# Matmuls of the seven-product chains issued as pairs of 64-column products in the two column halves

## The reference

```python
proj = h @ w_in + b_in                                     # both layers, first model
ff = jnp.square(jax.nn.relu(x @ w_up[l])) @ w_down[l]
x = layer_norm(ALPHA * x + ff, ln2_g[l], ln2_b[l])
...
y_b = ssd_mixer(z, xbc, dt_raw, ...) @ w_o_ssd             # second model
mix = (jax.nn.sigmoid(g_a) * y_a + jax.nn.sigmoid(g_b) * y_b) @ w_out
u_gate, u_up = jnp.split(h2 @ w_ffn_in, 2, axis=-1)
f = (jax.nn.silu(u_gate) * u_up) @ w_ffn_out
```

## Time and profile before

| | |
|---|---|
| median of three runs | 1318.59 us (1318.37 to 1318.83) |
| span of the profiled execution | 1316.3 us (the page gives no other time of it) |
| TensorE matmul / weight load busy | 1304.7 us (99%) / 1169.0 us (89%), 9133 of each |
| VectorE / ScalarE / GpSimd busy | 943.1 (72%) / 427.1 (32%) / 178.0 us (14%) |
| DMA | 242.39 MB, mean 184 GB/s |

### The profile page before, as it was taken

How to read it: one execution, slowest core, us unless ns; L and a number is a source line. 1 busy time by engine, 2 the same in 40 slices (tenths; PEclk the granted TensorE clock), 3 DMA queues, 4 the chain that set the end, 5 groups by cost and what they waited for, 6 DMA issues and landing times.

```text
span 1316.3 us, 22023 instructions
## 1 busy us (share of the span) xinstructions
PE 1304.7 (99%) x9133; PEld 1169.0 (89%) x9133; DVE 943.1 (72%) x1602; ACT 427.1 (32%) x929; POOL 178.0 (14%) x164
## 2 busy tenths in 40 slices
PE   9999999999999999999999999999999999999998
PEld 7975899988997599998877899999999986999987
DVE  4985798556688388956872898887897845865653
ACT  2254333220236333323055425464732103100101
POOL 3100322030000042204043000003100100011100
PEclk9999999999999999999999999999999999999999
DMA  9632577576533257767639895046635453545550
GB/s 327 196 129 96 192 247 266 213 270 220 183 107 127 96 195 278 254 225 265 215 80 253 226 248 161 18 167 216 195 129 192 171 182 129 192 150 171 176 175 33
DMA packets 132882, 242.39 MB, mean 184 GB/s; under 512 B 7237, under 2 KB 37725, under 8 KB 132273
## 3 DMA queue, kind: packets, MB, share of 16 engines
q1 hardware_dynamic: 122506, 218.00, 48.0%
q0 software_dynamic: 9872, 22.80, 7.2%
q10 hardware_dynamic: 407, 0.20, 0.1%
HBM read 231.49 MB, written 6.34 MB: 181 GB/s over the span
## 4 chain that ended last, share of the span: by engine, by line
PE 95%; DVE 2%; DMA 2%; issue 0%; SPq 0%; ACT 0%; DVEq 0%
PE acc L2192 58%; PE scr L2192 18%; PE pvw L2192 9%; PE ptb L2300 1%; PE pvw L2805 1%; PE scr L2798 1%; DMA hid<-in_x 1%; PE scr L2291 1%; PE ptb L2192 1%; DMA ring<-in_w_up 1%; PE pvw L2310 1%; PE ptb L2630 0%; PE pvw L2316 0%; DVE ring L1344 0%; PE scr L2775 0%
## 5 line engine op out<-in xcount | busy, mean ns | idle before, releaser
L2192 PE MATMUL acc<-y,ring 128*128 128x128 f32 (+2 forms) x1120 | 155.0, 294 | 0.0
L2192 PEld LDWEIGHTS acc<-y,ring 128*128 128x128 f32 (+1 forms) x1120 | 144.3, 191 | 8.0 <-issue 1.3
L2192 PE MATMUL acc<-ring,big 128*128 128x256 f32 (+1 forms) x376 | 115.5, 453 | 0.0
L2192 PEld LDWEIGHTS acc<-ring,big 128*128 128x128 f32 x376 | 70.6, 190 | 33.3 <-issue 26.9
L2192 PE MATMUL acc<-x,ring 128*128 128x128 f32 (+1 forms) x768 | 99.7, 284 | 0.0
L2192 PE MATMUL acc<-ring,hid 128*128 128x256 f32 (+1 forms) x364 | 98.8, 417 | 0.0
L2192 PEld LDWEIGHTS acc<-x,ring 128*128 128x128 f32 x768 | 93.7, 192 | 2.5 <-issue 1.0
L895 ACT ACTIVATE ring<-ring,silc 128x512 f32<-128x512 f32 x96 | 60.2, 712 | 96.1 <-DMA ring<-in_ada_w 96.1
L2192 PEld LDWEIGHTS acc<-ring,hid 128*128 128x128 f32 x364 | 68.4, 190 | 21.7 <-issue 14.3
L2192 PE MATMUL acc<-ysq,ring 128*128 128x128 f32 x624 | 75.8, 275 | 0.1
L2192 PEld LDWEIGHTS acc<-ysq,ring 128*128 128x128 f32 x624 | 72.6, 192 | 0.4 <-ACT ysq L1076 0.4
(11 more groups left out here) (581 smaller groups left out, 2781.2 us busy)
## 6 DMA issues: line engine op xcount, KB each, us to landing
ring<-in_w_in SPq DMA_DIRECT2D x24, 2048.0 KB, 11.2
ring<-in_w_up SPq DMA_DIRECT2D x16, 2048.0 KB, 8.6
ring<-in_w_down SPq DMA_DIRECT2D x16, 2048.0 KB, 8.0
ring<-in_ada_w SPq DMA_DIRECT2D x12, 2048.0 KB, 13.8
ring<-in_w_ffn_in SPq DMA_DIRECT2D x22, 1024.0 KB, 6.7
ring<-in_w_out SPq DMA_DIRECT2D x6, 2048.0 KB, 8.6
ring<-in_w_o_ssd SPq DMA_DIRECT2D x4, 2048.0 KB, 7.9
ring<-in_w_ffn_out SPq DMA_DIRECT2D x4, 2048.0 KB, 8.0
```

What stands on the lines that cost most here:

```text
L2192: ins = pe.matmul(dst, w, m, start=start, stop=stop, is_transpose=turned, skip_group_check=True)
```

## The change

In the branch of `product` that puts features on the partitions, each matmul is issued as two: weight columns 0 to 63 of the tile to output partitions 0 to 63, then weight columns 64 to 127 to partitions 64 to 127, both over the same 128 moving columns. The sums, the tiles, the semaphores and the order of all else stay. The branch `tokens=True` and `half_product` (another helper, of the second model's first products) are not changed.

```diff
+            def column_halves(dst, w, m, start, stop):
+
+                for c in (0, P // 2):
+                    ins = mm(dst[c:c + P // 2, :], w[:, c:c + P // 2], m, start, stop)
+                return ins
+
...
                     for k in range(kn):
                         if written is not None and i == 0:
                             pe.wait_ge(written[0], written[1] + k + 1)
-                        ins = mm(dst[:, i * P:(i + 1) * P], w[:, k, i * P:(i + 1) * P], a[:, k, :],
-                                 first and i == 0 and k == 0, last and k == kn - 1)
+                        ins = column_halves(dst[:, i * P:(i + 1) * P], w[:, k, i * P:(i + 1) * P], a[:, k, :],
+                                            first and i == 0 and k == 0, last and k == kn - 1)
```

## The result

| | before | after |
|---|---|---|
| median | 1318.48 us (1318.34 to 1318.83, 4 runs) | 1311.16 us (1310.79 to 1311.43, 4 runs) |
| span of the profiled execution | 1316.3 us | 1309.3 us |

The change makes the kernel 0.57% faster: the ratio is 0.9943, with a 95% interval from 0.9929 to 0.9957. The forecast was 1311.1 us.

A forecast was written before the change was run, and what follows sets the result against it. TensorE's own queue, busy 99% of the span, was taken as the bound, its product chains paced by weight loads. -12.6+0.6+4.5 = -7.5 us took the span from 1316.3 to 1308.8; plus 2.3, 1311.1 us, range 1306.5 to 1323.

The forecast's parts named there:

- Pairs: In the product chains, 5264 slots fall from 111.7 to 109.3 ns as two halves run at once: -12.6 us.
- What DVE doesn't let through: From 138.6 to 170.6 us the chain follows `w_up`'s landing and DVE's sums, so some 270 slots gain nothing: +0.6 us.
- Switches: On TensorE's queue, going between full-width and half-width matmuls costs about 0.15 to 0.197 us at new places: +4.5 us.
- Queue: 5264 more loads and matmuls on TensorE, with 42 more instruction blocks to fetch, stay hidden: costed at nothing.
- The sum: Over the profiled span: -12.6+0.6+4.5 = -7.5 us, from 1316.3 to 1308.8 us.
- the 2.3 that I added: The median of the runs before, 1318.59 us, stands 2.3 us above the profiled span; added to the predicted span.
- The rival that half loads share a bound: In product chains the slot stays at 111.7 ns and only switching costs are left: 1323.1 us, 12%.
- The rival that VectorE takes the place: In heads and FFN units, waits on DVE's sums (L1343 to L1346, L1284) eat gain: 1313.7 or 1316.4 us, 7%.
- The rival that pairing or queue fails in long chains: In long product chains a pair's slot grows, up to 218 ns and 1881 us, anything between possible; 4%.

The follow-up runs named there:

- `loads_alone`: The changed kernel with unused test chains of short full, half and quarter-width matmuls at the start of TensorE's queue; it grew by 28 us.
- the lean kernels: The kernels after and before the change, each without 8 of 30 convolution taps of the first model in both layers: 1308.38 and 1317.35 us.
- `head_full`: The changed kernel with the first model's head left at full width in both layers (672 slots): 1312.33 us.
- `one_full`: The changed kernel with the last of each product call's eight matmuls left at full width, 304 more switches each way: 1414.67 us.
- `quarters`: The changed kernel with each product-chain matmul issued as four calls of 32 weight columns instead of two of 64: 1478.49 us.
- `halves_apart`: The changed kernel with all four chunks of an output tile's lower half issued first, then all four of the upper: 1391.49 us.

## Why the prediction was right

1. *Pairs, -12.6 us.* Right in mechanism and size: 109.2 ns per slot in the chain, two half loads side by side in `loads_alone`. All of the 5264 slots got it, at nearer 2.5 than 2.4 ns: 5264 x 2.49 = -13.1.
2. *What DVE doesn't let through, +0.6 us.* Wrong in place and size. The stretch from 143 to 178 us, which I had taken off, gained 1.16 us, more than its slots alone, since its first weight sum took 1.23 us and not the 3.27 of the earlier trace rows. Waits came elsewhere: near 80 us behind the convolution taps, +0.57 (shown by the lean kernels and `head_full`), and at 929 us, +0.38, where the chain comes through ScalarE (L1105 to L1110) and VectorE. The weight sums, +0.94 in layer 1 and -0.39 in layer 0, are the race with GpSimd, which can fall either way in either kernel. With 0.33 of scatter in the first 22 us these steps add up to +1.8; some 1.0 of it is what the term meant. I had read VectorE's 24.79 of 25.00 us, and then looked for its price inside the head, where no wait stands; it was to be paid in the stage behind, where the softmax wants what the taps have delayed. That TensorE waited there already before, 0.57 us near 80 us, I hadn't seen either.
3. *Switches, +4.5 us.* Right: 0.15 in, 0.15 or 0.19 out, as many as counted. The side-by-side has 4.2, since a fourth entry, behind `decay_products` at 907 us, was hidden by a wait too, and leaving the L2523 matmul for halves costs 0.05 less. `one_full` gives 0.335 for a round trip.
4. *Queue, 0.* Right. The bound that I feared is there, in the fetch, but only at twice the rate (`quarters`).
5. *The sum.* -13.1+4.2+1.8 = -7.1 us for a span that fell by 7.0. The forecast of 7.5 was near because an error of 1.2 us in the second term met two of the other sign (0.5 and 0.3). That the time was hit within 0.1 us is luck on top: wherever time and span of one execution are both known, 2.0 us lie between them (1311.31 and 1309.3), so the 2.3 that I added held 0.3 by which the profiled execution was faster than its median. The next miss, 0.5 us in the span, was made up by it and by the median of the change, which lies 0.15 below its own profiled execution.

The rival that half loads share a bound, the one with the most chance, fell with `loads_alone`. The rival that VectorE takes the place was partly true, at about a third of its price and not on the sums that it named. The rival that pairing or queue fails in long chains fell too: a record with its load starts every 27.3 ns in `quarters`. The Trainium skill's rule that a load overlaps only matmuls of other row groups ("TensorE: Matmul & The Clock Gate", Part 3, "The mechanism") doesn't hold here: pairs in all rows run with their loads hidden, and the kernel before disagreed with it already, with full-width loads of 192 ns in slots of 111.7. The same section also lets a load go ahead when it targets the background weight buffer; these traces can't tell whether that is what happens.

What stays open: what makes that landing of `w_up` take 8.1 us in one execution and 9.0 in another, and so how often a kernel wins the race. With one trace of each kernel it can't be said whether the change shifts the odds.

## What to carry to other kernels

A full-width f32 matmul with 128 moving columns goes at the pace of its weight load; as two column halves it goes at the pace of its stream, 2% sooner. That pays only in long stretches of one width: a round trip costs what some 140 such slots gain, so look first at what stands between the chains, and turn that to the same width or leave short chains alone. And here, with TensorE 99% busy, the engine at 99% beside it took its share one stage later. Before a small difference between two profiles is put down to a change, look for places where two engines start within a few tenths of a microsecond of each other: one such order was worth 0.4 to 1.0 us here, as much as the waits that the change itself caused.

## What the hardware showed that I had not expected

- TensorE starts records of the idle column half ahead of earlier ones of the other half: with the partner eight records away, nine slots did the work of eight (`halves_apart`), not sixteen.
- Two half loads take half of a full one's time, 59 against 112 ns per slot at full clock, 107 against 213 at half clock (`loads_alone`).
- With 3.5 us per block of instructions TensorE runs dry, 123.5 us in all, while at 7 us it never did (`quarters`, and the change). Each of the 74 stops ends 1.2 to 1.6 us after a block's landing.
- A VectorE addition of 128x1024 took 1.22 us alone and some 3.3 us beside GpSimd additions of the same size; the order of two starts less than 0.5 us apart decided which.
